# Matmuls on zeros while x loads, a first projected tile in plain fp32, and GpSimd's constants behind the first head's values

## The reference, cut to what matters

```python
h = rmsnorm(x, norm_mix[0])                      # x * rsqrt(mean(x*x) + 1e-6) * gain
qkv = (h @ dsa_w_in).reshape(1, 256, 3, 3, 8, 128)    # 3 groups, (q, k, v), 8 heads of 128
# each group g: windowed attention with window, dilation = (128,1), (512,4), (2048,16)
# s = q k^T / sqrt(128) - slope * distance, masked; o = softmax(s) v
# the three groups' o are merged by their softmax weights; then x += o @ dsa_w_out
x += hier_moe(rmsnorm(x))                        # 32 experts, 2 MB per matrix and expert
x += (p[0] @ ple_w) * sigmoid(rmsnorm(x) @ ple_w_gate)
```

## Time and profile before

| | us |
|---|---|
| median of 3 runs | 1346.81 (1345.52 to 1347.76) |
| the profiled execution | 1347.4 |
| its span, first to last instruction | 1345.3 |
| PE busy (share of the span) | 1035.3 (77%) |
| PEld busy | 811.3 (60%) |
| DVE busy | 454.6 (34%) |
| ACT busy | 298.0 (22%) |
| POOL busy | 16.4 (1%) |
| read from HBM | 467.00 MB, 348 GB/s over the span |

### The profile page before, as it was taken

How to read it: one execution, slowest core, us unless ns; L and a number is a source line. 1 busy time by engine, 2 the same in 40 slices (tenths; PEclk the granted TensorE clock), 3 DMA queues, 4 the chain that set the end, 5 groups by cost and what they waited for, 6 DMA issues and landing times.

```text
span 1345.3 us, 31101 instructions
## 1 busy us (share of the span) xinstructions
PE 1035.3 (77%) x13816; PEld 811.3 (60%) x13816; DVE 454.6 (34%) x1005; ACT 298.0 (22%) x573; POOL 16.4 (1%) x25
## 2 busy tenths in 40 slices
PE   7999999988767666656676989988667657656667
PEld 7999999965545445444454756656444444534446
DVE  5545555562212111111212775522121111212127
ACT  5433444330100000000002754311000000000007
POOL 2000000000000000000000010000000000000000
PEclk9999999999988887888888999989788898888879
DMA  9996553599999999999999950899999999999991
GB/s 283 310 256 168 160 140 125 223 384 426 425 427 425 427 427 426 426 425 426 427 426 378 390 195 1 320 422 425 426 426 427 426 425 427 427 426 425 427 374 43
DMA packets 115817, 469.94 MB, mean 349 GB/s; under 512 B 4816, under 2 KB 79696, under 8 KB 90992
## 3 DMA queue, kind: packets, MB, share of 16 engines
q1 hardware_dynamic: 115008, 465.78, 86.8%
q0 software_dynamic: 688, 2.28, 0.4%
HBM read 467.00 MB, written 1.05 MB: 348 GB/s over the span
## 4 chain that ended last, share of the span: by engine, by line
DMA 52%; PE 40%; DVE 4%; ACT 2%; issue 2%; DVEq 0%; SPq 0%; ACTq 0%
DMA ring<-moe_w_down 28%; DMA ring<-moe_w_gate 13%; DMA ring<-moe_w_up 11%; PE ps L1868 6%; PE ps L1617 5%; PE ps L1618 5%; PE ps L1616 5%; PE ps L1891 4%; PE ps L1730 2%; PE ps L1755 1%; PE ps L1969 1%; PE ps L1680 1%; PE ps L1656 1%; ACT g_hi L860 1%; PE ps L1921 1%
## 5 line engine op out<-in xcount | busy, mean ns | idle before, releaser
L1868 PE MATMUL ps<-ring,scr 128*32 128x128 f32 x8192 | 284.5, 298 | 146.0 <-DMA ring<-moe_w_up 100.0
L1868 PEld LDWEIGHTS ps<-ring,scr 128*32 128x32 f32 x8192 | 247.3, 120 | 185.5 <-DMA ring<-moe_w_up 111.7
L1891 PE MATMUL ps<-ring,scr 128*32 128x256 f32 x1920 | 159.8, 487 | 117.6 <-DMA ring<-moe_w_down 105.0
L1891 PEld LDWEIGHTS ps<-ring,scr 128*32 128x32 f32 x1920 | 78.1, 134 | 180.2 <-issue 123.3
L825 ACT COPY scr<-ps 32x256 f32<-32x256 f32 x128 | 46.8, 365 | 544.9 <-PE ps L1891 544.1
L1308 DVE TENSOR_TENSOR scr<-scr,ps 128x128 f32<-128x128 f32 x64 | 23.8, 371 | 422.7 <-PE ps L1868 422.7
L1321 DVE COPY scr<-ps 32x256 f32<-32x256 f32 x128 | 53.3, 417 | 243.1 <-PE ps L1891 242.3
L1616 PE MATMUL ps<-a_hT_hi,w_qk_hi 128*128 128x256 f32 x368 | 104.4, 284 | 0.0
L1618 PE MATMUL ps<-a_hT_hi,w_qk_lo 128*128 128x256 f32 x368 | 103.8, 282 | 0.0
L1617 PE MATMUL ps<-hT_lo,w_qk_hi 128*128 128x256 f32 x368 | 103.6, 282 | 0.0
L1921 PE MATMUL ps<-scr 128*128 128x512 f32 x128 | 64.6, 651 | 15.4 <-DVE scr L1321 15.4
(11 more groups left out here) (283 smaller groups left out, 1195.1 us busy)
## 6 DMA issues: line engine op xcount, KB each, us to landing
ring<-moe_w_gate SPq DMA_DIRECT2D x64, 2048.0 KB, 36.5
ring<-moe_w_up SPq DMA_DIRECT2D x64, 2048.0 KB, 36.4
ring<-moe_w_down SPq DMA_DIRECT2D x60, 2048.0 KB, 36.8
ring<-dsa_w_in SPq DMA_DIRECT2D x72, 512.0 KB, 6.9
ring<-ple_w_gate SPq DMA_DIRECT2D x4, 2048.0 KB, 37.0
ring<-dsa_w_out SPq DMA_DIRECT2D x2, 2048.0 KB, 13.6
scr<-moe_w_down SPq DMA_DIRECT2D x4, 1024.0 KB, 7.3
scr<-moe_w_down SPq DMA_DIRECT2D x8, 512.0 KB, 9.5
```

Of the source, the lines that this page charges most:

```text
L1868: mm = pe.matmul(bank(b)[CW * q:CW * q + CW, 0:P], xT[:, k, :], tile(t, KD, FF)[:, k, P * q:P * q + P], start=(k == 0), stop=(k == KD - 1))
L1891: mm = pe.matmul(bank(6)[CW * q:CW * q + CW, 0:T], e_hT[:, CW * j:CW * j + CW], down[j][:, T * q:T * q + T], start=(j == 0), stop=(j == FF ...
```

## The change

- w_in is read with slice k holding the rows 128k + p instead of 8p + k (the gains of layer 0's first norm on the host likewise). The scaled x is then read contiguously.
- The product of the gains goes to a new place, `a_hT` (in the scratch that later holds the attention's output), so that its low part, at hT, no longer overwrites it.
- Tile 0 of head 0 is made of 16 plain fp32 matmuls on the weights as landed and `a_hT`; its casts and subtraction go, and the counts of `w_qk_high`, `w_qk_low` and `q_high` fall by one everywhere. Tile 1 takes the written-out form that tile 0 had, and the values one like it, pass by pass over both halves of the tokens.
- ACT scales both halves of the second chunk of x and DVE one half of the first alone.
- PE starts with 16 fp32 matmuls of 128x128 on a block of zeros that POOL writes first.
- POOL issues the constants when head 0's values have landed, not when the keys of g = 2 have.

```diff
+        a_hT = scratch(5760, KD, T)
+        warm = scratch(7808, P)
-        dsa_in_v = dsa_w_in.rearrange("(p k) (g w n) -> g p k w n", k=KD, g=GROUPS, w=3)
+        dsa_in_v = dsa_w_in.rearrange("(k p) (g w n) -> g p k w n", k=KD, g=GROUPS, w=3)
...
+            pool.memset(warm, 0.0).then_inc(S("fills"), 1)
             pool.dma_start(wts[:, :], gains).then_inc(S("wts_in"), 16)
...
-            pool.wait_ge(landed_dsa[GROUPS - 1], dsa_fills(0, 0, 2))
+            pool.wait_ge(landed_dsa[GROUPS], dsa_fills(0, 0, GROUPS))
...
+            first_root(0)
+            first_scale(0, 1).then_inc(S("hs_a"), 1)
+            first_root(1)
+            first_scale(1, 0).then_inc(S("hs_d"), 1)
+            first_scale(1, 1).then_inc(S("hs_a"), 1)
...
-            act.wait_ge(S("hT_turned"), 2)
+            act.wait_ge(S("hT_turned"), 4)
             high_hT(0, 0)
-            act.wait_ge(S("first_q_in"), 16)
-            act.copy(w_qk_hi[0][:, :, 0:DH], w_qk[0][0][:, :, 0:DH]).then_inc(S("q_high"), 1)
...
-            act.wait_ge(landed_dsa[0], 16)
-            act.copy(w_qk_hi[0][:, :, DH:2 * DH], w_qk[0][0][:, :, DH:2 * DH]).then_inc(S("w_qk_high"), 1)
...
-            for g in range(GROUPS):
+            for g in range(1, GROUPS):
                 low_qk(0, g, 0)
...
+            pe.wait_ge(S("fills"), 1)
+            for _ in range(16):
+                pe.matmul(bank(3)[:, 0:P], warm, warm, start=True, stop=True)
             for c in range(TC):
                 turn_rows(0, c)
+            pe.wait_ge(S("first_q_in"), 16)
+            for which in range(2):
+                if which == 1:
+                    pe.wait_ge(landed_dsa[0], 16)
+                for k in range(KD):
+                    if which == 0 and k % 4 == 0:
+                        pe.wait_ge(S("hT_ready"), TC + 1 + k // 4)
+                    mm = pe.matmul(bank(proj_bank(0, 0))[:, which * T:which * T + T], w_qk[0][0][:, k, which * DH:(which + 1) * DH],
+                                   a_hT[:, k, :], start=(which == 0 and k == 0), stop=(k == KD - 1), skip_group_check=True)
+            mm.then_inc(S("qk_ready"), 1)
...
+            project_qk(0, 2, 0, first=True)
+            pe.wait_ge(S("w_v_high"), 1)
+            for w, h in ((w_v_hi, a_hT_hi), (w_v_hi, hT_lo), (w_v_lo[0], a_hT_hi)):
+                if w is not w_v_hi:
+                    pe.wait_ge(S("w_v_low"), 1)
+                for c in range(TC):
+                    if w is w_v_hi and h is a_hT_hi:
+                        pe.wait_ge(S("qk_copied"), 2 + c)
```

More of the change, by code:

```diff
@@ L763, in step, with first_root, first_scale @@
                     act.copy(a_o_hi[:, 0:HEADS - 1, :], a_o[:, 0:HEADS - 1, :]).then_inc(S("o_high"), 1)
-            act.wait_ge(S("fills"), 2)
+            act.wait_ge(S("fills"), 3)
             table(ACT.Sqrt)
-            for c in range(TC):
-                norm_chunk(0, c)
+            def first_root(c):
+                square(0, c)
+                act.wait_ge(S("var_ready"), c + 1)
+                act.activation(root[:, c:c + 1], root[:, c:c + 1], ACT.Sqrt, scale=1.0 / D).then_inc(S("root_ready"), 1)
+                act.wait_ge(S("rstd_ready"), c + 1)
+            def first_scale(c, b):
+                return act.activation(hs[:, c, 4 * b:4 * b + 4, :],
+                                      x_sb[:, c, 512 * b:512 * b + 512].rearrange("p (k t) -> p k t", t=P),
+                                      ACT.Copy, scale=rstd[:, c:c + 1])
+            first_root(0)
[3 more added lines that the diff above has]
+            first_scale(1, 1).then_inc(S("hs_a"), 1)
             def high_hT(c, b):
@@ L771, in high_hT @@
                 blocks = slice(4 * b, 4 * b + 4)
-                return act.copy(by_chunk(a_hT_hi[:, blocks, :], c), by_chunk(hT[:, blocks, :], c))
-            act.wait_ge(S("hT_turned"), 2)
+                return act.copy(by_chunk(a_hT_hi[:, blocks, :], c), by_chunk(a_hT[:, blocks, :], c))
+            act.wait_ge(S("hT_turned"), 4)
             high_hT(0, 0)
-            act.wait_ge(S("first_q_in"), 16)
-            act.copy(w_qk_hi[0][:, :, 0:DH], w_qk[0][0][:, :, 0:DH]).then_inc(S("q_high"), 1)
-            act.wait_ge(S("hT_turned"), 4)
             high_hT(0, 1).then_inc(S("hT_high"), 1)
@@ L1069, in low_qk @@
             def low_qk(h, g, par):
-                dve.wait_ge(S("w_qk_high"), GROUPS * h + g + 1)
+                dve.wait_ge(S("w_qk_high"), GROUPS * h + g)
                 dve.tensor_tensor(w_qk_lo[par][g], w_qk[par][g],
@@ L1133, in step @@
                 copy_v(h_proj, buf, first)
[L1135 to L1138, removed]
+            square(0, 0)
+            roots(0, 0, 1)
+            dve.tensor_scalar(hs[:, 0, 0:4, :], x_sb[:, 0, 0:512].rearrange("p (k t) -> p k t", t=P), rstd[:, 0:1], None,
+                              ALU.mult).then_inc(S("hs_d"), 1)
+            square(0, 1)
+            roots(0, 1, 2)
             for c in range(TC):
@@ L1461, in low_queries @@
             def low_queries(n):
-                dve.wait_ge(S("w_qk_high"), GROUPS * HEADS + n + 1)
+                dve.wait_ge(S("w_qk_high"), GROUPS * HEADS + n)
                 cols = slice(512 * n, 512 * n + 512)
@@ L1620, in project_qk @@
             def project_qk(h, g, buf, first=False):
-                pe.wait_ge(S("w_qk_low"), GROUPS * h + g + 1)
+                pe.wait_ge(S("w_qk_low"), GROUPS * h + g)
                 if g == 2:
@@ L1691, in step @@
                 project_v(h_proj, buf)
+            pe.wait_ge(S("fills"), 1)
+            for _ in range(16):
+                pe.matmul(bank(3)[:, 0:P], warm, warm, start=True, stop=True)
             for c in range(TC):
                 turn_rows(0, c)
+            pe.wait_ge(S("first_q_in"), 16)
[8 more added lines that the diff above has]
+            mm.then_inc(S("qk_ready"), 1)
             pe.wait_ge(S("hT_high"), TC)
-            pe.wait_ge(S("q_high"), 1)
-            for w, h in ((w_qk_hi[0], a_hT_hi), (w_qk_hi[0], hT_lo), (w_qk_lo[0][0], a_hT_hi)):
+            pe.wait_ge(S("w_qk_high"), 1)
+            for w, h in ((w_qk_hi[1], a_hT_hi), (w_qk_hi[1], hT_lo), (w_qk_lo[0][1], a_hT_hi)):
                 if h is hT_lo:
                     pe.wait_ge(S("hT_low"), TC)
-                if w is not w_qk_hi[0]:
+                if w is not w_qk_hi[1]:
                     pe.wait_ge(S("w_qk_low"), 1)
                 for which in range(2):
-                    if w is w_qk_hi[0] and h is a_hT_hi and which == 1:
-                        pe.wait_ge(S("w_qk_high"), 1)
                     for k in range(KD):
-                        first = w is w_qk_hi[0] and h is a_hT_hi and which == 0 and k == 0
-                        last = w is not w_qk_hi[0] and k == KD - 1
-                        mm = pe.matmul(bank(proj_bank(0, 0))[:, which * T:which * T + T],
+                        first = w is w_qk_hi[1] and h is a_hT_hi and which == 0 and k == 0
+                        last = w is not w_qk_hi[1] and k == KD - 1
+                        mm = pe.matmul(bank(proj_bank(0, 1))[:, which * T:which * T + T],
                                        w[:, k, which * DH:(which + 1) * DH],
@@ L1714, in _ @@
             mm.then_inc(S("qk_ready"), 1)
-            for g in range(1, GROUPS):
-                project_qk(0, g, 0, first=True)
-            project_v(0, 0)
+            project_qk(0, 2, 0, first=True)
[6 more added lines that the diff above has]
+                        pe.wait_ge(S("qk_copied"), 2 + c)
+                    for k in range(KD):
+                        mm = pe.matmul(bank(proj_bank(0, GROUPS + c))[:, 0:GROUPS * DH], h[:, k, c * P:(c + 1) * P], w[:, k, :],
+                                       start=(w is w_v_hi and h is a_hT_hi and k == 0), stop=(w is not w_v_hi and k == KD - 1),
+                                       skip_group_check=True)
+                    if w is not w_v_hi:
+                        mm.then_inc(S("v_ready"), 1)
             step(0, 1, 1, first=True)
@@ L2041, in project_q @@
             def project_q(c, ns):
-                pe.wait_ge(S("q_high"), c + 2)
-                pe.wait_ge(S("w_qk_low"), GROUPS * HEADS + ns[-1] + 1)
+                pe.wait_ge(S("q_high"), c + 1)
+                pe.wait_ge(S("w_qk_low"), GROUPS * HEADS + ns[-1])
                 b = 4 if c == 0 else 0
@@ L2224 @@
         "gains": np.ascontiguousarray(np.concatenate(
-            [g.reshape(KD, P).T if n % 3 == 2 or n == 3 else g.reshape(P, KD) for n, g in enumerate(gains)]
+            [g.reshape(KD, P).T if n % 3 == 2 or n % 3 == 0 else g.reshape(P, KD) for n, g in enumerate(gains)]
             + [a["mla_q_norm"].reshape(-1, P).T, a["mla_kv_norm"].reshape(-1, P).T]
```

6 lines of the change are left out of this document (3 added, 3 removed).

## The result

The changed kernel takes 1350.22 us (median of 20 executions, 1348.50 to 1353.10); the kernel before, on the same chip, 1348.20 (20 executions). The ratio is 1.0015, 95% interval 1.0009 to 1.0021: some 2 us slower, where 3.4 us faster was forecast. The profiled execution took 1350.38, its span is 1348.4.

What follows compares the result with a forecast made beforehand. TensorE was taken to set the pace to about 280 us, the weight stream after. First score: 15.95 + 19.74 + 0.55 + 0.4 = 36.6 against 40.02, 3.4 us earlier, so 1346.8 - 3.4 = 1343.4 us; range 1341.8 to 1346.9.

Steps and rivals of the forecast that it cites:

- The slower rival: Start: new row order slows the w_in loads; 20% costs 1.0 us, 30% gives 1350.0; chance 0.07.
- wait for VectorE (0.55): Head 0, tile 2: TensorE comes at 21.55 but VectorE's low part is ready at 22.1, a 0.55 us wait.
- the 0.4 forecast for the values: Head 0's values, second half: TensorE waits 0.25 to 0.65 us, taken as 0.4, for ScalarE's copy of tile 2.
- the prediction's own 10.1 to 11.1: Tile 0's start: third gain product done by 11.1 at the latest, perhaps up to 1 us sooner.
- tile 1's start: Head 0: tile 1 starts at 15.95, when ScalarE's cast ends, with tile 0 hidden behind it at 14.9.
- the danger in the values: Head 0's values: tile 2's copy stands behind head 1's cast; without later constants a 3.4 us stall, chance 0.10.
- nothing on TensorE needs them for 11 us: VectorE's copies of head 0's values come after 37.7, some 0.6 us later relative to TensorE; cost taken as 0.
- neither clock rival: Start: clock lost before tile 0 (1344.8, chance 0.08) or after it, in tile 1 (1344.6, chance 0.18).
- the first rival: Clock lost before tile 0: tile 0 runs low, ends 17.9 instead of 15.95; loss 1.4 us, 1344.8, chance 0.08.

Runs made afterwards that it cites:

- 7 zero matmuls: Changed kernel with 7 matmuls on zeros of 256 columns in place of 16 of 128, 36 TensorE instructions fewer: 1344.38 us, ratio 0.9977 to the kernel before.
- the two with dead code behind the same start: Changed kernel with 110 or 16 never-executed transpositions in layer 0's jumped-over overflow block: 1351.45 us (ratio 1.0025) and 1353.73 us (1.0035).
- the two with dead code: Kernel before with 18 or 8 never-executed transpositions in layer 0's jumped-over overflow block: 1352.92 us (ratio 1.0040) and 1348.23 us (1.0003).

## Why the prediction was wrong

**The step that failed** is in the first part: "whatever TensorE gains before 280 us moves the whole weight stream by the same amount, and the end with it". The first half held: -2.2 in the changed kernel's trace and -3.0 with 7 zero matmuls, unchanged over 235 us of heads, and found again at 720 to a few tenths. The second half took the rest of the kernel as rigid. It is, in what it computes, but not in where its code lies. I counted what each edit adds in time and in queues, not in instructions; none of the rivals had the code's length in it. The two stops, 2.81 and 2.37 us, are more than the gain. The forecast itself, 3.4 us, came out as 3.1 in the kernel that has the change without the stops. The slower rival that I did give (row order) had another mechanism: windows of 12 to 14 us show 291 GB/s in the kernel with 7 zero matmuls, against 290; the changed kernel's profiled execution alone showed 207 and 183 there (the two with dead code behind the same start 284 to 302), and its landings were 0.6 to 1.9 late.

**Tile 0** was mis-sized: 7.14 us at the full clock, where 3.7 was summed and 7.4 given as the bound for half the clock. (By doubling, an estimate, it would be 14.3 at half the clock; with half the clock in its first 3.7 us it took 8.95.) The row that I took as eight fp32 matmuls of 512 columns has four, recorded twice each: 3.70/4 = 0.93 for 512 columns, 0.46 for 256; tile 0's sixteen took 7.14/16 = 0.45 each. Tile 1 therefore came at 17.07 instead of 15.95, and tile 2 did not wait for VectorE (0.55). Of the 0.4 forecast for the values nothing came in that kernel; in the changed kernel their first pass took 3.18 instead of 2.94, 0.24 more.

**The sum at the first score**: 36.6 forecast, 37.03 with 7 zero matmuls, 37.46 in the changed kernel. Three errors nearly cancelled, which was luck: +1.1 for tile 1's start, -0.55 and -0.4 for the waits that it covered; the rest is within tenths. With 7.14 for tile 0 from the prediction's own 10.1 to 11.1, tile 1 would have begun at 17.2 to 18.2 and the sum been 37.0 to 38.0. No run has tile 0 in its old form or the old row order with the rest of the change, so what these two are worth by themselves isn't shown.

**Held**: zeros from 1.1 and transpositions not held up; tile 2's copy as the danger in the values and the later constants as its cure (2.1 us, shown by putting them back); values' and head 1's weights at 22.57 and 27.34 against 23.3 and 26.9 to 27.3. VectorE's copies, of which I wrote that nothing on TensorE needs them for 11 us, are needed at once by head 1's products: they cost 0.4 in the changed kernel's profiled execution, whose loads were late, and nothing with 7 zero matmuls or with dead code behind the same start.

**The clock.** I took from one execution that transpositions raise it. Other executions of the same start don't repeat that: the rise came at 11.0 in the earlier trace rows, at 16.1 with the constants alone moved, and at 17.9 and 18.3 in the two with dead code, and there tile 0's matmuls had long begun. Without zeros it came at 14.4, within tile 0. So I had too little to set the rule aside (the Trainium skill, "TensorE: Matmul & The Clock Gate", "Part 4: PE-mode transpose", that transpose mode doesn't count as busy in the same way): four of five starts fit it and the one that I read doesn't, which leaves it open. What is shown is that in all seven traces with zeros the rise comes at 3.9 to 5.3. In six of them the clock then stays up beyond 280 us, so that neither clock rival came about. In the seventh, with half of tile 0, it fell during tile 0, which there began 0.6 later, after 0.93 us idle instead of 0.33: the first rival is not far off.

## What to carry to other kernels

Count the instructions that an edit adds on each engine with a long jump, as well as its microseconds; a kernel that skips a never-taken block of code can win or lose 5 us of 1348 by 36 instructions ahead of it or in it. When a start-up gain is gone at the end, lay the two traces against each other instruction by instruction: a shift that is constant over the heads, is found again 440 us later and then turns in one step names the place. A cost per instruction is taken from a row only after its count has been held against the loop in the code.

## What the runs showed of the hardware

- A piece of code fetched behind the jump in layer 0 let TensorE go on 6.26 to 6.34 us after the jump: 3.8 until the transfer began, 1.1 for it, 1.4 until the next instruction. In layer 1 it was 4.85 and 5.85, with 2.3 and 3.3 until the transfer began. With the target not held the jump itself lasted 6.2 to 6.35, and 4.1 in layer 1, instead of 0.35, and the stop was 3.8 to 3.9, with the clock at 0.50 behind it.
- A plain fp32 matmul is recorded as two and takes 0.45 us for 256 columns; the one-pass form 0.12 to 0.13 (2.07/16). For one tile the plain form costs 7.14 against three passes of 2.1, and pays only by the cast and the subtraction that it saves.
- The granted clock of a window ahead of the first recorded change reads 1.00, whatever it is: 1.00 in 5 to 10 us without the zeros, where a transposition took 1.94/8 = 0.243.
